# Where PE takes its slab within an attention step

## The reference

```
sc = einsum('bhcqd,bhckd->bhcqk', qi, kh)            # c: the two maps of a head
p  = softmax(where(kpos <= qpos, sc, -1e30))
w  = p[:, :, 0] - lam * p[:, :, 1]
out = einsum('bhqk,bhkv->bhqv', w, vh)               # dimension 128
```

## Time and profile before

| what | value |
|---|---|
| timed runs | 2315.69, 2326.36 and 2315.44 us; median 2315.69 |
| profiled execution | 2325.52 us on the device, span 2323.7 us |
| PE busy | 2188.7 us, 94% of the span, 10064 matmuls |
| DVE, ACT, POOL busy | 805.7, 794.0 and 875.7 us |
| chain that ended last | PE 85%, DVE 10%, ACT 2%, issue 1% |
| loads | 190.96 MB, mean 82 GB/s |

### The profile page before, as it was taken

How to read it: one execution, slowest core, us unless ns; L and a number is a source line. 1 busy time by engine, 2 the same in 40 slices (tenths; PEclk the granted TensorE clock), 3 DMA queues, 4 the chain that set the end, 5 groups by cost and what they waited for, 6 DMA issues and landing times.

```text
span 2323.7 us, 24860 instructions
## 1 busy us (share of the span) xinstructions
PE 2188.7 (94%) x10064; PEld 1773.0 (76%) x10064; DVE 805.7 (35%) x1411; ACT 794.0 (34%) x1407; POOL 875.7 (38%) x436
## 2 busy tenths in 40 slices
PE   5999999988767789999999999999999999999998
PEld 5888888865444678888878888888888888788886
DVE  2111102785555241111032676332113565632112
ACT  3222223324433342222143444332223445333222
POOL 2444443432111224445424443334444343334442
PEclk9999999987776899999999999999999999999999
DMA  4333332420000123333323222223333222223332
GB/s 139 105 92 100 99 91 91 137 72 1 0 1 0 55 75 98 100 94 97 99 91 114 79 68 72 73 91 100 93 107 114 82 73 73 73 77 97 96 95 73
DMA packets 231538, 190.96 MB, mean 82 GB/s; under 512 B 6400, under 2 KB 192256, under 8 KB 231168
## 3 DMA queue, kind: packets, MB, share of 16 engines
q1 hardware_dynamic: 231424, 189.37, 26.8%
HBM read 187.25 MB, written 2.10 MB: 81 GB/s over the span
## 4 chain that ended last, share of the span: by engine, by line
PE 85%; DVE 10%; ACT 2%; issue 1%; DMA 0%; SPq 0%; DVEq 0%; ACTq 0%
PE bank L1337 27%; PE bank L1338 26%; PE bank L1339 26%; PE bank L1331 3%; PE bank L1507 1%; DVE pt_lo L1102 1%; PE bank L1508 1%; DVE p_tok L1056 1%; PE bank L1610 1%; DVE qk_tok L991 1%; DVE t_sin L985 1%; DVE p_tok L1069 1%; DVE t_cos L980 1%; DVE xn L910 1%; ACT junk L598 1%
## 5 line engine op out<-in xcount | busy, mean ns | idle before, releaser
L538 POOL TENSOR_TENSOR w_lo<-w_raw,w_hi 128x1024 fp32r<-128x1024 f32 x326 | 789.1, 2432 | 1047.0 <-ACT w_hi L578 1046.1
L1337 PE MATMUL bank<-xt_hi,w_hi 128*128 128x512 f32 (+1 forms) x1376 | 531.6, 386 | 15.3 <-DVE xt_lo L939 14.9
L1338 PE MATMUL bank<-xt_lo,w_hi 128*128 128x512 f32 (+1 forms) x1376 | 528.0, 384 | 0.0
L1339 PE MATMUL bank<-xt_hi,w_lo 128*128 128x512 f32 (+1 forms) x1376 | 527.8, 384 | 0.0
L578 ACT ACTIVATE w_hi<-w_raw 128x1024 fp32r<-128x1024 f32 x326 | 342.1, 1054 | 299.1 <-DMA w_raw<-in_ffn_w_down 144.6
L1337 PEld LDWEIGHTS bank<-xt_hi,w_hi 128*128 128x128 f32 x1376 | 261.5, 190 | 66.6 <-DVE xt_lo L939 16.0
L1339 PEld LDWEIGHTS bank<-xt_hi,w_lo 128*128 128x128 f32 x1376 | 261.2, 190 | 50.7
L1338 PEld LDWEIGHTS bank<-xt_lo,w_hi 128*128 128x128 f32 x1376 | 261.6, 190 | 48.8
L1337 PE MATMUL bank<-w_hi,xt_hi 128*128 128x512 f32 (+1 forms) x624 | 245.3, 393 | 3.4 <-DVE xt_lo L1085 2.8
L1338 PE MATMUL bank<-w_lo,xt_hi 128*128 128x512 f32 (+1 forms) x624 | 240.8, 386 | 0.0
L1339 PE MATMUL bank<-w_hi,xt_lo 128*128 128x512 f32 (+1 forms) x624 | 240.7, 386 | 0.0
(11 more groups left out here) (242 smaller groups left out, 2995.5 us busy)
## 6 DMA issues: line engine op xcount, KB each, us to landing
w_raw<-in_w_in SPq DMA_DIRECT2D x132, 512.0 KB, 3.7
w_raw<-in_ffn_w_down SPq DMA_DIRECT2D x44, 512.0 KB, 3.6
w_raw<-in_ffn_w_gate SPq DMA_DIRECT2D x43, 512.0 KB, 3.7
w_raw<-in_ffn_w_up SPq DMA_DIRECT2D x43, 512.0 KB, 3.7
w_raw<-in_w_out SPq DMA_DIRECT2D x24, 512.0 KB, 3.6
w_raw<-in_w_branch SPq DMA_DIRECT2D x24, 512.0 KB, 3.3
w_raw<-in_w_qkv SPq DMA_DIRECT2D x16, 512.0 KB, 3.6
x_tok<-in_x SPq DMA_DIRECT2D x4, 512.0 KB, 7.4
```

What stands on the lines that cost most here:

```text
L538: pool.tensor_tensor(lo_slots[i], raw_slots[i], f32(hi_slots[i]), ALU.subtract).then_inc(lo_ready, 1)
L1337: pe.matmul(out_ap, ah, bh, start=first, stop=False)
L1338: pe.matmul(out_ap, ah, bl, start=False, stop=False)
L1339: return pe.matmul(out_ap, al, bh, start=False, stop=last)
```

## The change

In PE's list of an attention step the slab (or, in steps 16 and 17, the convolution slab) stands behind the transposes and the values instead of ahead of them. No other engine's list is touched.

```diff
                         ins.then_inc(s2_done, 1)
-                        token_slab(fill + i, c, bank[0:4], filler_free(h))
-                    else:
-                        if i == 16:
-                            pe.wait_ge(nm2_done, 16 * (l + 1))
-                        feature_tile(conv + i - 16, bank[4 + i - 16][:, :])
                     if 1 <= i <= 16:
                         m = n - 1
                         pe.wait_ge(w2_done, m + 1)
...
                             ins = three(bank[7][:, cols(m % 2)], (pt2_hi[:, m % 2, cols(j)], pt2_lo[:, m % 2, cols(j)]),
                                         (va_hi[:, j, cols(mh)], va_lo[:, j, cols(mh)]), j == 0, j == mc)
                         ins.then_inc(o2_done, 1)
+                    if i < 16:
+                        token_slab(fill + i, c, bank[0:4], filler_free(h))
+                    else:
+                        if i == 16:
+                            pe.wait_ge(nm2_done, 16 * (l + 1))
+                        feature_tile(conv + i - 16, bank[4 + i - 16][:, :])
                     if i == 16:
```

## The result

The changed kernel took 2349.77 us (median of four runs, 2346.89 to 2357.25) against 2319.57 for the kernel before beside it (2315.44 to 2326.36). The ratio is 1.0132 with a 95% interval of 1.0093 to 1.0172. In a later job (e8) the same two kernels gave 1.0107 (1.0082 to 1.0133). The change is slower, as forecast. But 2349.8 lies above the range, which ended at 2347, and the rise is larger than the forecast one: 20.5 us were forecast, the medians differ by 30.2, and the profiled executions differ by 27.1 us (span 2350.8 against 2323.7). Two of the four single runs, at 2346.9, lay just inside the range. Two executions of the later jobs, one of the kernel before (2779.9 us) and one of e4_step17 (2782.1 us), ran at a granted clock of 0.74 and are left out of all figures.

A forecast was written before the change was run, and what follows sets the result against it. PE's own work was taken to bound the attention stage. Its new waits less the 0.83 us won came to 10.26 us per layer, twice 20.5, which put on the median 2315.7 gave 2336.2 us; range 2327 to 2347.

The forecast's parts named there:

- step 1: At the first step's transposes, PE waits 0.94 us per layer for DVE's combined probabilities.
- steps 4 and 8: Ends of heads 0 and 1, four-chunk steps: PE's transposes wait 1.31 us each, behind ACT's evacuation of the slab.
- step 11: Three-chunk step of the third head: PE waits 1.45 us for DVE's chain, which includes a rotation.
- step 12: Four-chunk step of the third head: PE waits 2.09 us for DVE's chain, which includes a rotation.
- step 16: No scores left, four extra low halves (L1161) in DVE's chain: PE waits 3.63 us at the transposes of step 15.
- step 17: Values of step 15, now ahead of the second convolution slab, wait 0.36 us for their low half.
- the 0.83 won: PE's wait before the retention loop, behind the last value product, disappears: 0.83 us won per layer.
- The clock falls: Rival: waits of 2.09 and 3.63 us lower the granted clock in attention, 6.6 us more, 2342.8; chance 0.2.
- its race: Rival: DVE's L1204 starts ahead of POOL's L538 everywhere, each chain 2.05 us shorter, 2325.8; chance 0.1.
- Not slower: Rival: the edges win 0.10 us in all 32 steps and the chains are covered, 2312.5; chance 0.04.
- the edges: Where PE changes from one kind of work to another: 0.10 us won or lost per step, ±3.2 us, taken as 0.
- The evacuation: Rival: ACT's evacuation ends 0.5 us earlier at four heads' ends, 2 us less, 2334; no chance of its own.

The follow-up runs named there:

- e4_step17: Kernel before with only step 17 in the new order, the values ahead of the second convolution slab; ratio 0.9986 to the kernel before.
- e1_warm: Changed kernel with PE's waits in steps 4, 8, 12 and 16 filled by matmuls whose results are unused; ratio 1.0091 to the kernel before.
- e6: Changed kernel with ACT taking the transposes' high half ahead of the slab group's four evacuations in four-chunk steps; ratio 1.0106 to the kernel before.
- e5: Changed kernel with DVE's four rotations of rqk in steps 8, 9, 12 and 13 in place of 8 to 11; ratio 1.0090 to the kernel before.
- e3: Kernel before with the slab placed last only in steps 16 and 17; ratio 1.0043 to the kernel before.
- e7: Changed kernel with the changes of e5 and e6, and step 16 back in the old order; ratio 1.0028 to the kernel before.
- the heads alone: Changed kernel with steps 16 and 17 back in the old order, so the slab is last only in steps 0 to 15; ratio 1.0083 to the kernel before.

## Why the prediction was wrong

*The waits* were right, place by place. Predicted and measured: step 1 0.94 and 0.85, steps 4 and 8 1.31 and 1.27, step 11 1.45 and 1.51, step 12 2.09 and 2.00, step 16 3.63 and 3.67, step 17 0.36 and 0.37 (an idle time of 0.15), and the 0.83 won. The sum of 10.26 us per layer stands against 10.44 in the first layer of e1_warm, where the clock stayed up. Splitting the waits by cause was right too: ACT's evacuation at steps 4 and 8 (e6), the rotation at 11 and 12 (e5), the chain by way of the four L1161 at step 16 (e3).

*The step that failed* is the clock: the sum has no term for it. "The clock falls" was a rival with a chance of 0.2, argued down because PE is dense on both sides and at 1.00 around a wait of 0.83 us. Ten of ten waits of 3.6 us brought it down on just such ground. In the two stages the clock took 8.0 us (28.9 less 2 x 10.44), in five falls, so about 1.6 us a fall. The row at 779 us had shown that price, 1.66 (the granted clock from 779.07 to 782.82 is 0.54); behind step 12 the slab took 7.21 in place of 5.61 us. What the rival had wrong is the number: it counted four falls, behind the waits of 2.09 and 3.63 us, and the fifth stood behind one of 1.27. Its 27.1 us in all are just what the two spans differ by, but that is luck: the stages differ by 28.9, and 1.7 us went the other way ahead of them. The mistake was to weigh a short wait (0.83) as evidence for a wait four times as long, when the one row with a wait of nearly that length showed a fall.

*The base* added the rest, and without it the range would have held. The sum was put on 2315.7, the median of three runs of which one was 2326.4; with a fourth run the kernel before came to 2319.6 beside the changed one, 3.9 us more. So of the 13.6 us by which 2336.2 was missed, 8.0 are the clock, 3.9 the base, and 1.7 are not accounted for, less than four runs can tell. With the clock alone the forecast would have been 2344, inside the range. In the two later jobs the kernel before had medians of 2323.7 and 2325.6 in 16 and 17 runs. Its runs differ by their clock: in the last job those below 2319 us had a mean granted clock of 0.963 to 0.966, those above 2325 us 0.956 to 0.960. To say that nothing depends on which run the sum starts from was wrong, then: a range around a sum that is known to the microsecond must still hold the scatter of its base, here 11 us between the fastest and the slowest of three runs.

*The other rivals.* POOL did not lose its race: L1204 of step 4 lasted 0.35 and of step 0 2.38 us in the kernel after, as the earlier trace rows. The sum of that rival took 2.05 us off the third head's chains as well, but L1204 was short there already (0.62 us in step 10); the long instruction is L1142. "Not slower" is out by the result, and by e7, where the edges gave nothing. The evacuation did not end earlier: steps 4 and 8 waited 1.27 us for a predicted 1.31.

## What to carry to other kernels

When the engine that sets the time is fully busy, work placed between a request and its use is cover: list the chain from the request to the use, subtract what is left between them, and the wait follows, here within a tenth of a microsecond at all seven places. Then price PE's idleness twice, once for the wait and once for the clock behind it; here that second price was about a quarter of the first with the heads alone (3.2 of 13.9 us) and two fifths with the whole change (8.0 of 20.9). Where a wait can't be avoided, filling it with matmuls whose result nobody reads kept the clock at 1.00 here (e1, no fall behind any of the eight filled waits), and so did waits made short: none of 24 waits under 0.9 us was followed by a fall. Whether one long wait could be split into short ones wasn't tried.

## What was not expected of the hardware

The five falls in the third row of the table stand behind four waits of 1.27 us and one of 1.54, with PE dense around them. Other waits of the same length at the same steps were followed by none. Which of them falls is not settled by these runs: the same kernel had two falls in the first layer in one trace and one in another. And 14 matmuls of 256 columns, issued only to keep PE busy, cost no time (2.54 us from the scores to the transposes, 2.55 without them), and no fall followed the filled 2 us of step 12 in either layer; unfilled, six of eight such waits had one.
